# One load of 8 MB for an expert's up weights in an encoder kernel with 32 experts

## The reference, cut to what matters

```python
h2 = rmsnorm(x, norm2_g)
logits = h2 @ w_router + b_router            # (256, 32)
top_v, top_i = top_k(logits, 4); gates = softmax(top_v)
# for each of the 32 experts e, over the tokens routed to it:
gu = xblk @ w_gu[e] + b_gu[e]                # w_gu[e]: 1024 x 2048 floats, 8 MB
gate, up = minimum(gu[:, :1024], 7), clip(gu[:, 1024:], -7, 7)
act = (up + 1) * (gate * sigmoid(1.702 * gate))
y = act @ w_down[e] + b_down[e]              # w_down[e]: 1024 x 1024 floats, 4 MB
```

## Time and profile before

| | |
|---|---|
| Time, median of 3 runs | 1134.76 us (1134.4 to 1135.06) |
| Time of the profiled execution | 1134.09 us |
| Its span, first to last instruction | 1132.3 us |
| Mean granted TensorE clock | 0.991 of full speed |
| TensorE busy | 1091.9 us (96%) |
| Moved by DMA | 434.61 MB, mean 384 GB/s |

### The profile page before, as it was taken

How to read it: one execution, slowest core, us unless ns; L and a number is a source line. 1 busy time by engine, 2 the same in 40 slices (tenths; PEclk the granted TensorE clock), 3 DMA queues, 4 the chain that set the end, 5 groups by cost and what they waited for, 6 DMA issues and landing times.

```text
span 1132.3 us, 12526 instructions
## 1 busy us (share of the span) xinstructions
PE 1091.9 (96%) x5278; PEld 482.5 (43%) x5279; DVE 223.8 (20%) x549; ACT 125.4 (11%) x271; POOL 30.3 (3%) x43
## 2 busy tenths in 40 slices
PE   7999999999999999999999999999999999999996
PEld 5858887443333333333333333333333333333332
DVE  1264213331111111111111121111111111111112
ACT  1053111210000000000000010000000000000001
POOL 1250000000000000000000000000000000000000
PEclk9999999999999999999999999999999999999999
DMA  9934366399999999999999999999999999999995
GB/s 362 411 144 168 130 222 233 144 396 421 432 432 432 429 431 433 431 432 433 432 431 431 435 428 429 439 428 429 438 428 431 435 429 431 434 429 431 417 421 232
DMA packets 31484, 434.61 MB, mean 384 GB/s; under 512 B 6944, under 2 KB 7200, under 8 KB 9440
## 3 DMA queue, kind: packets, MB, share of 16 engines
q1 hardware_dynamic: 26960, 430.33, 90.1%
q10 hardware_dynamic: 4496, 3.87, 1.1%
HBM read 433.14 MB, written 1.05 MB: 383 GB/s over the span
## 4 chain that ended last, share of the span: by engine, by line
PE 65%; DMA 32%; DVE 1%; ACT 1%; issue 0%; POOL 0%; DVEq 0%; SPq 0%; POOLq 0%
DMA ring<-in_up 32%; PE ps L1352 26%; PE ps L1366 11%; PE ps L1172 5%; PE ps L1300 3%; PE ps L1374 3%; PE ps L1186 2%; PE ps L1249 2%; PE ps L1061 2%; PE ps L1361 2%; PE ps L1116 1%; PE ps L1080 1%; PE ps L1051 1%; PE ps L1336 1%; PE ps L1330 1%; PE ps L1089 1%
## 5 line engine op out<-in xcount | busy, mean ns | idle before, releaser
L1352 PE MATMUL ps<-ring,work 128*64 128x512 f32 x2048 | 470.7, 605 | 20.2 <-DMA ring<-in_up 20.2
L1352 PEld LDWEIGHTS ps<-ring,work 128*64 128x64 f32 x2048 | 141.8, 138 | 317.8 <-issue 283.8
L1366 PE MATMUL ps<-ring,work 128*64 128x512 f32 x1024 | 226.8, 595 | 1.6 <-DVE work L977 1.6
L918 DVE TENSOR_SCALAR work<-ps 128x512 f32<-128x512 f32 x32 | 22.1, 691 | 698.1 <-PE ps L1352 698.1
L1366 PEld LDWEIGHTS ps<-ring,work 128*64 128x64 f32 x1024 | 70.6, 137 | 133.7 <-issue 128.0
L1300 PEld LDWEIGHTS ps<-work 128*128 128x128 f32 x512 | 61.8, 191 | 24.0 <-issue 22.7
L1300 PE MATMUL ps<-work 128*128 128x128 f32 x512 | 70.3, 281 | 0.5 <-DVE work L904 0.5
L1374 PE MATMUL ps<-work 64*128 64x512 f32 x264 | 65.6, 615 | 0.7 <-ACT work L658 0.7
L1172 PE MATMUL ps<-work,ring 128*128 128x256 f32 x256 | 56.6, 379 | 0.0
L631 ACT ACTIVATE work<-ps 128x256 f32<-128x256 f32 x33 | 12.7, 383 | 355.5 <-PE ps L1336 355.5
L1172 PEld LDWEIGHTS ps<-work,ring 128*128 128x128 f32 x256 | 48.5, 190 | 6.6
(11 more groups left out here) (157 smaller groups left out, 520.9 us busy)
## 6 DMA issues: line engine op xcount, KB each, us to landing
ring<-in_up SPq DMA_DIRECT2D x52, 4096.0 KB, 45.2
ring<-in_down SPq DMA_DIRECT2D x26, 4096.0 KB, 44.1
ring<-in_up SPq DMA_DIRECT2D x48, 1024.0 KB, 10.8
ring<-in_down SPq DMA_DIRECT2D x24, 1024.0 KB, 10.6
ring<-in_front SPq DMA_DIRECT2D x22, 1024.0 KB, 17.2
ring<-in_front SPq DMA_DIRECT2D x2, 832.0 KB, 7.5
ring<-in_x SPq DMA_DIRECT2D x2, 512.0 KB, 4.2
ring<-in_x ACTq DMA_DIRECT2D x1, 1024.0 KB, 4.8
```

Of the source, the lines that this page charges most:

```text
L918: return dve.tensor_scalar(up_c, ps[:, UP, :], LIMIT, -LIMIT, ALU.min, ALU.max)
L1352: last = pe.matmul(ps[n * CAP:(n + 1) * CAP, bank, :], x, w[bank - GATE][:, n * BANK:(n + 1) * BANK], start=k == 0, stop=k == KT - 1, skip ...
L1366: last = pe.matmul(ps[n * CAP:(n + 1) * CAP, Y, :], lhs(actT, k), w[:, n * BANK:(n + 1) * BANK], start=k == 0, stop=k == KT - 1, skip_grou ...
```

## The change

In turns 2 to 14 the up weights of an expert come in one load of eight slots, 8 MB, with a row of 64 KB for each partition; the down weights stay one load of four slots. A turn has four loads where it had six. `UNITS` lists the first slot and the number of slots of each. SyncE waits until all slots of a unit are free, and TensorE waits for a unit at its first slot. The up weights are laid out in HBM as 128 rows of 64 KB for each expert, so that a fine load of an up slot takes 8 KB from each of 128 rows of 64 KB. The loads of the further rounds are two for each expert in place of three.

```diff
+UNITS = ((0, 8), (8, 4), (12, 8), (20, 4))
...
-    ups = w_gate_up.reshape(E, KT // SPAN, SPAN, P, 2 * F).transpose(0, 1, 3, 2, 4).reshape(-1, P, SPAN * SLOT)
+    ups = w_gate_up.reshape(E, KT, P, 2 * F).transpose(0, 2, 1, 3).reshape(-1, P, UP_SLOTS * SLOT)
...
-        grouped = [sem(f"group_loaded{g}") for g in range(RING // SPAN)]
+        grouped = [sem(f"group_loaded{g}") for g in range(len(UNITS))]
...
             def unit(i, g):
-                u, j = divmod(g, PER_EXPERT // SPAN)
-                if j < UP_SLOTS // SPAN:
-                    return up_rows[:, bass.ds(i * (PAIR * UP_SLOTS // SPAN) + (u * UP_SLOTS // SPAN + j), 1), :]
-                return down_rows[:, bass.ds(i * (PAIR * DOWN_SLOTS // SPAN) + (u * DOWN_SLOTS // SPAN + j - UP_SLOTS // SPAN), 1), :]
+                rows = (up_rows, down_rows)[g % 2]
+                return rows[:, bass.ds(i * PAIR + g // 2, 1), :]
             def expert_load(i, at):
-                g, part = divmod(at, SPAN)
+                g = max(n for n, (first, _) in enumerate(UNITS) if first <= at)
+                part = at - UNITS[g][0]
...
             def group_load(i, g):
-                sp.wait_ge(freed, i * RING + (N_FRONT - RING + SPAN * (g + 1)))
-                sp.dma_start(ring[:, SPAN * g:SPAN * (g + 1), :], unit(i, g)).then_inc(grouped[g], 16)
+                first, count = UNITS[g]
+                sp.wait_ge(freed, i * RING + (N_FRONT - RING + first + count))
+                sp.dma_start(ring[:, first:first + count, :], unit(i, g)).then_inc(grouped[g], 16)
...
             with sp.Fori(2, TURNS - 1) as i:
-                for g in range(RING // SPAN):
+                for g in range(len(UNITS)):
                     group_load(i, g)
...
+            starts = [first for first, _ in UNITS]
...
-                        elif at % SPAN == 0:
-                            pe.wait_ge(grouped[at // SPAN], i * (16 * UNROLL // PAIR) + 16 * (pair - 1))
+                        elif at in starts:
+                            pe.wait_ge(grouped[starts.index(at)], i * (16 * UNROLL // PAIR) + 16 * (pair - 1))
```

More of the change, by code:

```diff
@@ L422, in _ @@
                             k = sp.snap(done)
-                            row, low = sp.snap(e * (UP_SLOTS // SPAN)), sp.snap(e * (DOWN_SLOTS // SPAN))
+                            row = sp.snap(e * 1)
                             sp.reg_add(done, done, 1)
                             sp.wait_ge(scattered, k + 1)
[L427 to L431, removed]
+                            sp.dma_start(ring[:, 0:UP_SLOTS, :], up_rows[:, bass.ds(row, 1), :]).then_inc(v_loaded, 16)
+                            sp.dma_start(ring[:, UP_SLOTS:PER_EXPERT, :], down_rows[:, bass.ds(row, 1), :]).then_inc(v_loaded, 16)
                         sp.nop()
@@ L1464, in _ @@
                             turn_gated(0).then_inc(v_gTd, 1)
-                            pe.wait_ge(v_loaded, k * (16 * PER_EXPERT // SPAN) + 16 * PER_EXPERT // SPAN)
+                            pe.wait_ge(v_loaded, k * 32 + 32)
                             for j in range(KT):
```

## The result

The changed kernel takes 1144.85 us (median of four runs, 1144.43 to 1146.07) where the kernel before takes 1134.76 (four runs, 1134.4 to 1135.06): a ratio of 1.0094, 95% interval [1.0082, 1.0106]. It is slower by 10.1 us. The profiled execution took 1144.43 us, its span is 1142.5.

The account below looks back on a forecast made before the run. The end was taken to be set by when the weight stream's last loads land and how far TensorE is behind them. 5.2 + 6.9 - 0.2 - 1.8 = +10.1 us on 1134.8 gave 1144.9 us, range 1140.5 to 1149.0.

Parts of the forecast that it names:

- Fewer loads: Turns 2 to 14: 26 loads fewer for the same bytes, each saving 0.07 us of overhead, -1.8 us.
- The bound of no saving: In the 26 saved loads: nothing gained if 64 KB rows go out as two 32 KB pieces that carry the overhead.
- The late start: First 8 MB load, issued at 302.70 us to an empty queue, lands at 324.3 instead of 319.1, +5.2 us.
- TensorE's lag: At expert 29 four up slots of matmuls come after the landing, +6.9 us; later waits vanish, -0.2 us.
- The clock: Half clock after the wait before expert 29 would add 1.7 us; 4 in 10, not in the sum.
- Where TensorE begins to wait: In the loop: TensorE's lead shrinks 2.3 us per expert and is gone at expert 12, about 557 us.
- A: Rival on the 8 MB loads: wide rows carry more, 19.0 us per load, total 1136.0 us; 4 in 100.
- B: Rival on load cost: each load pays a 2.2 us start-up, 57 us for 26 loads, total 1090; 2 in 100.
- C: Rival on the HBM layout: rows of 64 KB are read worse, 2.1% slower up loads, total 1157.2; 6 in 100.
- D: Rival on the first wide load or TensorE's lag: late start hidden or lag repaid, 1139.7 us; 4 in 100.

Follow-up runs that it names:

- whole_in_middle: The changed kernel with turns 2, 3 and 12 to 14 in loads of 4 MB, 8 MB up loads only in turns 4 to 11; 1133.32 us, ratio 0.9989.
- late_first_issue: The kernel before, but SyncE waits once, ahead of turn 2, until eight slots are free instead of four; 1139.89 us, ratio 1.0055.
- pe_waits_whole: The kernel before, but TensorE waits at a grouped expert's first up slot for both 4 MB up loads; 1140.79 us, ratio 1.0068.
- fours_first: The changed kernel with turns 2 and 3 in loads of 4 MB, whole units from turn 4 to 14; 1139.76 us, ratio 1.005.
- after_again: The changed kernel run once more, unaltered, on the chip of the last four runs; 1145.66 us, ratio 1.01 against the kernel before.
- early_half: The changed kernel, but its first 8 MB load (expert 4) goes out as two 4 MB halves, the first once four slots are free; 1142.89 us, ratio 1.0077.
- wide_rows_only: The kernel before with up weights in HBM rows of 64 KB, still loaded in groups of four slots and slot by slot; 1134.32 us, ratio 1.0002.

## Why the prediction was right

The mechanism held: a late start, a lag at expert 29 and a small saving, added up. That the time of 1144.9 us was met within 0.1 us is luck: two errors of more than a microsecond, one each way, stood behind it, and the same kernel gave 1145.66 on another chip. Step by step:

- *Fewer loads.* Reckoned -1.8 us. In the changed kernel's chain the up loads land at 587.34 (545.15 + 42.19) and at 1052.51 (1010.33 + 42.18), eight turns apart: 58.15 us for a turn, as forecast, against 58.29 before. That makes 8 MB take 19.36 us, against 19.37 reckoned. The bound of no saving (rows cut in two) is excluded by this and by the packet count. whole_in_middle can't confirm the price of a load, for the reason given there.
- *The late start.* Reckoned +5.2, with a landing at 324.3; it came at 325.9, against 319.1 before: +6.8. The place, the cause and the 3.4 us from the last landing to the issue were right; the term was 1.6 us too small, because over an empty queue 8 MB take 23.5 us and not 21.6 (the issue itself came 0.3 us earlier than before, as all of that execution did). Of the excess 0.3 us are the start of a 4 MB load (2.5 us, not 2.2); what makes the rest is open. late_first_issue shows the same with the packets of before.
- *What gave it back.* Expert 29 landed at 1052.5 instead of 1048.75: +3.75, where the sum had 5.2 - 1.8 = 3.4. With 6.8 and -1.8 it should have been 5.0. The missing 1.2 us are single landings: in the kernel before, the one at 969.46 + 50.2 = 1019.6 is 0.87 us late and one at 377.6 is 0.2 late, and neither delay is in the changed kernel; there the first down load lands 9.56 us after the up load and not 9.71. That adds up to 1.2. The prediction had passed over these and took every load at 9.715. Such single delays are met at different places in different kernels, so this part of the match is luck; that they have the same cause as the 1.4 us extra at the start is argued from the traces and not shown.
- *TensorE's lag.* Reckoned +6.9 - 0.2; pe_waits_whole alone gives +7.0. fours_first takes 6.4 us more than whole_in_middle, although it has 6 loads fewer, worth an estimated 0.4 us. In the two main traces the last group of matmuls starts 10.4 us later (1132.95 against 1122.56), and the landing at expert 29 gives 3.75 of that; 6.65 are left for the lag. Shown.
- *The clock.* In the profiled execution of the changed kernel no half-clock stretch followed the wait before expert 29. In that of after_again one did, of the size given (12.20 us for the 48 instructions in place of 10.52), and in that of early_half as well. So the forecast without this term was met in one execution by its absence and in the other by an earlier stream. The prediction also names only three of the long waits in its chain. The same chain of the kernel before has four more groups of 16 matmuls in 5.35 us, at 814.78, 873.07, 931.36 and 989.65; this is the last of them:

```profile
989.65 5.35 PE ps L1352 x16
```

  With them five of the seven long waits in the chain are followed by half clock, so 4 in 10 was low by its own rows.
- *Where TensorE begins to wait.* Reckoned about 557 us, on expert 12; the first wait is at 529 us, on expert 11. The late start is 1.6 us later, and the sum was rounded: 29.14 - 26.77 is 2.37 us for an expert and not 2.3, by which the lead of 16.3 us is gone at expert 11 already. All its waits for weights in the loop:

```profile
PE ps L1350 <- DMA ring<-in_up: 31.4, 19, 2.2
```

- *The rivals.* A and B fall with 19.36 us for 8 MB. C falls with wide_rows_only. D, a start without a gap, would have been 1139.7, +4.9; fours_first, in which just that is arranged, has +5.2. Its end behind the last matmuls is some 0.9 us shorter, so the two figures agree better than the trace bears out.

## What to carry to other kernels

Where a stream of loads bounds the kernel, as here, the overhead of a load (0.07 us) may be the smallest part of what its size costs. The larger part comes from the two waits that it makes coarser: the loader's, which decides whether the queue ever runs dry, and the consumer's, which decides how far it is behind when the last data lands. In these runs coarse units cost nothing where the queue was long and there was time to catch up (whole_in_middle), so keep fine ones where the queue is short (after a start-up phase) and for as many steps ahead of the end as the consumer needs to repay one unit; a unit's worth of lag divided by the consumer's gain per step estimates their number (6.9 / 2.3 = 3 experts here; two more experts gave back 4 us, six gave back all of it, and three were not tried). Where a gap is mended, set every later issue against the stream as it would then be, or the gap only moves on.

## What the runs showed of the hardware

A row of 64 KB travels as one packet (3328 packets fewer for 26 loads). In a full queue a load of 1, 4 or 8 MB lands 2.48, 9.71 or 19.36 us after what stands before it; for 1 and 4 MB this holds with a row pitch of 32 and of 64 KB. A load into an empty queue lands 2.2 us later than its transfer alone takes for 1 MB and 2.5 for 4 MB, but 4.1 for 8 MB; about the same (3.9) shows when the 8 MB come as two loads. A wait of TensorE of about 2.1 us was followed by a stretch at half clock in some places and not in others, even in two executions of the same kernel (1052.64 in the one, 1051.15 in the other), and cost 1.7 us where it was. The Trainium skill (DMA: Bandwidth & Descriptors, "Anatomy of one DMA — SWDGE (gpsimd) path") gives about 2.0 us of fixed cost for each DMA that GpSimd issues. The loads here are issued by SyncE: alone in the queue they show 2.2 to 2.5 us for 1 and 4 MB, near that figure, and in a full queue 0.07 us. The prediction set the same figure against these loads without that difference.
